# Attention's inverse sums through one 128-column operand, layer 1's map preparation one slot later, the head's tiles in another order

## The chip, the core and the metric

The kernel runs on one core of a Trainium2 chip. Its engines each work through their own list of instructions in order: TensorE (PE) multiplies, VectorE (DVE), ScalarE (ACT) and GpSimd (POOL) work on elements, and SyncE (SP) starts transfers. They meet through semaphores. The metric is the device time of one execution in microseconds (us); 0.2% of it is about what a measurement can tell from no change.

## What is computed

Two layers of a bidirectional encoder over 512 tokens of 1024 channels, in float32. A layer has an attention branch and a state-space branch, both gated, and a feed-forward part (FFN). Cut to what the change touches:

```python
def attend(qi):                       # 8 heads, QK_DIM 96, V_DIM 64
    s = jnp.einsum('bqhd,bkhd->bhqk', qi, k, preferred_element_type=jnp.float32) * scale
    p = jax.nn.softmax(s, axis=-1)
    return jnp.einsum('bhqk,bkhv->bqhv', p.astype(v.dtype), v)

for l in range(DEPTH):                # DEPTH = 2
    ...                               # projections, gates, attention -> branch_a
    y = _s5_bidir(u, ssm_lam_re[l], ssm_lam_im[l], ssm_log_dt[l], ssm_b_re[l], ssm_b_im[l],
                  ssm_c_re[l], ssm_c_im[l], ssm_d[l])
    ...                               # -> branch_b
    x = x + (gate_a * branch_a + gate_b * branch_b) @ w_o[l]
    x = x + _swiglu(_rmsnorm(x, norm2_g[l]), w_ffn_gate[l], w_ffn_up[l], w_ffn_down[l])
```

## The kernel before

**Products.** A float32 product is done as three matmuls (`products`, L1713 to L1715) of high parts and remainders in fp32r. Weights come as slabs of 512 KB: SP loads a slab into `stage`, ACT copies it to `wh` (L603), POOL writes the remainder to `wl` (L511). Transposes and a few small products run in plain float32, where the profile records two passes per matmul.

**Attention.** Four pairs of heads (`hp`), eight units (`u`) a pair: a unit is one head and one block of 128 queries. PE first makes the projected tiles, `qkv_tile(hp, t)`, four a pair (L1984 to L1991). The four transposes `turn(0, i)` of the first pair stand between the tiles of pair 2 and those of pair 3; they wait for POOL's `rotated()` (semaphore `q_ready`) and for the keys. ACT copies each tile (`raw`), and takes roots (`root`); DVE squares and sums, inverts, writes the remainders `turned(0, i)`, then `squares(3)`, and then takes the first maximum.

Then a loop over `a = 8*hp + u` (L1999). In step `a` PE makes the scores of unit `a` (three matmuls), turns the next pair's q and k at `u` 3 to 6 (L1980), transposes the probabilities of unit `a-2` (L2027), and at odd steps multiplies two units' probabilities with the values (L2056, L2057). DVE takes the maximum `nmx` (L1605), the remainder `pTl` (L1621) and others; ACT the exponential `prob` (L1020), the high part `pTh` and others. At `u == 0` DVE inverts the eight sums of the pair that ended (`prc`, L1616). At `u == 1` PE spreads them over bank 6: eight matmuls, each with one column of `prc` broadcast to 64 weight columns and the identity as the moving operand (L2036). ACT copies bank 6 to `Rn` at `u == 2` (`scales`), and POOL scales the output.

POOL's own list in that loop: at `u == 7` `v_rest` (L545, which waits for ACT's `vh_ready`), at `u == 0` of the next pair four products into `rt`, which lies in the tile `SS` (L535), at `u == 1` the two sums L539 and L540, a drain that raises `q_ready`, and the keys `normed_keys` (L552, L555).

**Layer 1's state-space maps** are prepared during layer 0's FFN, in 38 slots: `prepare(l, at)` is called on DVE, ACT and PE after each of the 11 gate/up blocks and each of the 8 output tiles of the two halves. The slots of block of channels `b` follow from `PREP_AT[b]` = 9, 14, 19, 24: DVE's `input_powers` part 0 (L1235 to L1238) in the slot itself, part 1 and `output_powers` part 0 (L1240 to L1284) in the next, `output_powers` part 1 (L1289 to L1294) in the one after, then PE's transposes (L1726) three and four slots on, and the taps (L1741) five on. `input_powers` of block 0 first waits for the store of `TRa` to DRAM (`tr_stored`), which ACT starts in slot 9. Slot 10 follows the last gate/up block of the first half, k = 10. DVE's work of a gate/up block is two products (L1683, L1685), `hid` (L1688) and `hidl` (L1691); PE's output tile m = 0 needs all eleven `hidl`. From m = 2 on, an output tile waits for DVE's addition into `X` (L1700) two tiles back (`x_part`).

Of the kernel before, what the change touches and what calls it, by code (L numbers as in the profile page):

```python
# [12 lines left out]
P = 128  # L13
D_MODEL, SEQ, DEPTH = 1024, 512, 2
HEADS, QK, NOPE, ROPE, VD = 8, 96, 64, 32, 64
# [31 lines left out]
PREP_AT = tuple(9 + 5 * b for b in range(BLOCKS))  # L47
# [31 lines left out]
def build(nc, xT, stream, gcols, gqk, grows, dskip, params, cmat, rope, ident_in, out):  # L79
    with ExitStack() as ctx:  # L80
# [165 lines left out]
        rt = SS[:].rearrange("p (o t h q) -> p o t h q", o=4, t=TT, h=2)  # L246

# [84 lines left out]
        prc_ready = sem("prc_ready")  # L332
        k_normed = sem("k_normed")
# [168 lines left out]
        def _(pool):  # L502
# [11 lines left out]
            for l in range(0, DEPTH):  # L514
# [61 lines left out]
                for a in range(STEPS + 1):  # L576
                    hp, u = a // UNITS, a % UNITS

                    if a < STEPS and hp + 1 < PAIRS:
                        if u == 0:  # L580
                            rotated_products()
                        if u == 1:
                            rotated()
                            normed_keys(hp + 1)
                    elif a < STEPS and u in (2, 4, 6):
                        remainder(SLABS * l + S_UP + u // 2 - 1)
# [14 lines left out]
        def _(act):  # L601
# [149 lines left out]
            def prepare(l, at):  # L751
# [8 lines left out]
                if at == PREP_AT[0]:  # L760
                    store_turns(l)
# [12 lines left out]
            for l in range(0, DEPTH):  # L774
# [214 lines left out]
                for i in range(3 * TT):  # L989
                    raw(i)  # L990
                    if i // TT == 1:
                        squared(i)
                    if i == 5:
                        root(0, 1)
                    if i == 8:
                        v_high(0)
                    if i == 11:
                        root(1, 2)
                for i in range(4):
                    turned(0, i)  # L1000
                for i in range(3 * TT, PAIRS * TT):
                    raw(i)
                for a in range(STEPS + 2):
# [9 lines left out]
                    if a < STEPS:  # L1013
# [4 lines left out]
                        if hp >= 2 and u == 0:  # L1018
                            act.wait_ge(prc_ready, PAIRS * l + hp - 1)
                        act.activation(prob[e][:], ps[:, a % 2, :], ACT.Exp, bias=nmx[:, e:e + 1],  # L1020
                                       accum_out=psm[:, hp % 2, u:u + 1]).then_inc(exp_ready, 1)
                    if a == 4:
                        root(2, PAIRS)
# [9 lines left out]
                    if a >= UNITS and u == 2:  # L1033
                        scales(hp - 1)
# [72 lines left out]
        def _(dve):  # L1107
# [229 lines left out]
            for l in range(0, DEPTH):  # L1337
# [250 lines left out]

                squares(0)
# [9 lines left out]
                for a in range(STEPS + 2):  # L1599
# [17 lines left out]
                    if 2 <= a < STEPS + 2:  # L1617
# [4 lines left out]
                           pTh[o].bitcast(F32), SUB).then_inc(pT_ready, 1)  # L1622
                    if a < STEPS and hp and u == 5:
                        added(hp - 1, 1)
# [85 lines left out]
        def _(pe):  # L1710
# [48 lines left out]
            for l in range(0, DEPTH):  # L1759
# [224 lines left out]
                for hp in range(3):  # L1984
                    for t in range(TT):
                        qkv_tile(hp, t)
# [3 lines left out]
                for t in range(TT):  # L1990
                    qkv_tile(3, t)  # L1991
# [7 lines left out]
                for a in range(STEPS + 4):  # L1999
# [30 lines left out]
                    if a > UNITS and u == 1:  # L2030
# [209 lines left out]
```

## Time and profile before

| | us |
|---|---|
| median of 3 runs | 1555.11 (1554.45 to 1556.94) |
| the profiled execution's own time | 1559.6 |
| its span | 1557.8 |
| PE busy in it | 1520.7 (98%) |
| DVE busy | 872.3 (56%) |
| ACT busy | 601.9 (39%) |
| POOL busy | 579.4 (37%) |

Busy shares are averages over stages. In attention all of PE, DVE and ACT are nearly full; in the FFN PE alone is, save where DVE also prepares layer 1. An idle stretch is read from the engine's own rows: a row of the timeline gives start, duration, engine, line, operation, and in brackets how long the engine sat idle before it and which instruction released it. In such a row `x16` merges sixteen records. Only PE's idle time, and what makes PE slower, can be worth time here.

### The profile page before, as it was taken

What the parts mean: (1) busy time and instruction counts of PE and PEld (TensorE: products, weight loads), DVE (VectorE), ACT (ScalarE), POOL (GpSimd) and SP (SyncE); (2) the same over time, 40 slices, a digit from 0 to 9 for tenths busy, and PEclk for the clock granted to TensorE, in tenths of its full rate; (3) what the DMA queues carried; (4) which work ended last, traced back from release to release, by engine and by line L of the source; (5) the groups of instructions that cost most, each with busy time, mean ns of one, the idle gap of its engine ahead of it and who ended that gap; (6) DMA issues with size and microseconds to landing.
All of it is one profiled execution on the core that took longest, in us unless ns stands there. A gap on an engine that the chain in (4) does not pass through costs nothing.

```text
span 1557.8 us, 20874 instructions
## 1 busy us (share of the span) xinstructions
PE 1520.7 (98%) x8216; PEld 1204.1 (77%) x8216; DVE 872.3 (56%) x1224; ACT 601.9 (39%) x1017; POOL 579.4 (37%) x298
## 2 busy tenths in 40 slices
PE   8999999999999979999999999899999999999999
PEld 3545887878788858788788888787887888888887
DVE  5999877677448876756222971686763222012210
ACT  4554158742442222233332222787334222122220
POOL 0000043454443444354443323445444444443441
PEclk9999999999999989999999999999999999999999
DMA  6568710232232344343528532003223222222222
GB/s 242 165 209 299 276 61 1 69 108 78 90 132 82 118 153 138 121 158 110 163 85 300 207 127 93 28 1 102 100 84 101 89 97 94 94 95 95 95 95 81
DMA packets 73200, 188.32 MB, mean 121 GB/s; under 512 B 23568, under 2 KB 32144, under 8 KB 69008
## 3 DMA queue, kind: packets, MB, share of 16 engines
q1 hardware_dynamic: 41664, 144.13, 27.2%
q10 hardware_dynamic: 31440, 42.87, 8.6%
q8 instruction: 65, 1.06, 0.3%
q14 instruction: 31, 0.25, 0.0%
HBM read 154.47 MB, written 32.51 MB: 120 GB/s over the span
## 4 chain that ended last, share of the span: by engine, by line
PE 76%; DVE 12%; DVEq 5%; ACT 3%; issue 2%; DMA 1%; POOLq 0%; SPq 0%; POOL 0%; ACTq 0%
PE ps L1713 22%; PE ps L1715 22%; PE ps L1714 22%; PE ps L1862 2%; PE ps L2027 1%; DVE work L1115 1%; PE ps L1768 1%; PE ps L1839 1%; DVEq L1295 1%; PE ps L2036 1%; PE ps L2056 1%; PE ps L1807 1%; PE ps L2057 1%; DVEq L1242 1%; ACT prob L1020 1%
## 5 line engine op out<-in xcount | busy, mean ns | idle before, releaser
L511 POOL TENSOR_TENSOR wl<-stage,wh 128x1024 fp32r<-128x1024 f32 x204 | 510.4, 2506 | 872.9 <-ACT wh L603 676.6
L603 ACT ACTIVATE wh<-stage 128x1024 fp32r<-128x1024 f32 x210 | 220.3, 1055 | 320.9 <-PE ps L1715 221.7
L1713 PE MATMUL ps<-xg2h,wh 128*128 128x512 f32 x704 | 279.9, 398 | 0.0
L1715 PE MATMUL ps<-xg2h,wl 128*128 128x512 f32 x704 | 278.4, 395 | 0.0
L1714 PE MATMUL ps<-xg2l,wh 128*128 128x512 f32 x704 | 278.4, 395 | 0.0
L1713 PEld LDWEIGHTS ps<-xg2h,wh 128*128 128x128 f32 x704 | 132.3, 188 | 32.6 <-issue 0.9
L1714 PEld LDWEIGHTS ps<-xg2l,wh 128*128 128x128 f32 x704 | 132.3, 188 | 32.1 <-issue 0.5
L1715 PEld LDWEIGHTS ps<-xg2h,wl 128*128 128x128 f32 x704 | 132.2, 188 | 31.9
L1713 PE MATMUL ps<-hidh,wh 128*128 128x512 f32 x352 | 140.7, 400 | 10.0 <-DVE hidl L1691 9.3
L1714 PE MATMUL ps<-hidl,wh 128*128 128x512 f32 x352 | 139.9, 398 | 0.0
L1715 PE MATMUL ps<-hidh,wl 128*128 128x512 f32 x352 | 139.9, 397 | 0.0
L1700 DVE TENSOR_TENSOR X<-X,ps 128x512 f32<-128x512 f32 x32 | 21.9, 688 | 160.2 <-PE ps L1715 159.8
L1685 DVE TENSOR_TENSOR act<-ps,RS 128x512 f32<-128x512 f32 x44 | 30.3, 689 | 139.4 <-PE ps L1715 139.4
L1768 PE MATMUL ps<-X,slabs 128*128 128x512 f32 x224 | 102.0, 610 | 6.0 <-DMA X<-in_xT 5.1
L603 ACT ACTIVATE hidh<-hid 128x512 fp32r<-128x512 f32 x44 | 27.8, 632 | 164.0 <-DVE hid L1688 164.0
L1768 PEld LDWEIGHTS ps<-X,slabs 128*128 128x128 f32 x224 | 42.5, 194 | 58.7 <-issue 48.4
L1713 PEld LDWEIGHTS ps<-hidh,wh 128*128 128x128 f32 x352 | 66.7, 189 | 26.9 <-DVE hidl L1691 9.7
L1713 PE MATMUL ps<-xgh,wh 128*128 128x512 f32 x208 | 84.4, 406 | 0.0
L1715 PE MATMUL ps<-xgh,wl 128*128 128x512 f32 x208 | 82.3, 396 | 0.0
L1714 PE MATMUL ps<-xgl,wh 128*128 128x512 f32 x208 | 82.3, 395 | 0.0
L1715 PEld LDWEIGHTS ps<-hidh,wl 128*128 128x128 f32 x352 | 66.6, 189 | 16.2
L1714 PEld LDWEIGHTS ps<-hidl,wh 128*128 128x128 f32 x352 | 66.7, 190 | 15.9
(275 smaller groups left out, 2780.4 us busy)
## 6 DMA issues: line engine op xcount, KB each, us to landing
stage<-in_stream SPq DMA_DIRECT2D x210, 512.0 KB, 3.2
CPTR<-ctd_scr ACTq DMA_DIRECT2D x6, 1664.0 KB, 8.1
slabs<-in_stream SPq DMA_DIRECT2D x17, 512.0 KB, 5.7
InT<-in_scr ACTq DMA_DIRECT2D x6, 1024.0 KB, 6.4
ctd_scr<-CPp SPq DMA_DIRECT2D x4, 1152.0 KB, 8.0
ctd_scr<-CPp ACTq DMA_DIRECT2D x4, 1152.0 KB, 6.6
in_scr<-BPI SPq DMA_DIRECT2D x4, 1024.0 KB, 5.1
in_scr<-BPI ACTq DMA_DIRECT2D x4, 1024.0 KB, 3.9
```

Source lines behind the costliest of these rows:

```text
L511: pool.tensor_tensor(wl[:, s, :], stage[:, (n - RAW) % STAGES, :], wh[:, s, :].bitcast(F32), ALU.subtract).then_inc(wl_ready, 1)
L603: return act.activation(o, i, ACT.Copy, **kw)
L1020: act.activation(prob[e][:], ps[:, a % 2, :], ACT.Exp, bias=nmx[:, e:e + 1], accum_out=psm[:, hp % 2, u:u + 1]).then_inc(exp_ready, 1)
L1115: tt(t[0], a[1], b[1], MUL)
L1242: dve.drain()
L1685: tt(act2[:], ps[:, 5 + 2 * b, :], RS[:], MUL).then_inc(ffn_free, 1)
L1700: last = tt(X[:, m, :], X[:, m, :], ps[:, m % 2, :], ADD)
L1713: pe.matmul(o, wt[0], x[0], start=start, stop=False)
L1714: pe.matmul(o, wt[0], x[1], start=False, stop=False)
L1715: return pe.matmul(o, wt[1], x[0], start=False, stop=stop)
L1768: return pe.matmul(o, raw_slab(n)[:, k * P:(k + 1) * P], X[:, k, :], start=start, stop=stop)
L1862: last = pe.matmul(ps[:, 6 + gi, q * NCH:(q + 1) * NCH], CP[h, r, 2 * q + d, at:at + P], S[h, r, 2 * q + d, :], start=False, stop=(d == 1 ...
```

## The change

It has three parts.

1. **Inverse sums.** For the first three pairs of a layer DVE writes a tile `prw`, [128, 4, 128], in the memory of `SS`: `ones` times `prc`, each inverse sum spread over 64 columns, both heads side by side. It does so at `u == 1`, after `pTl`, behind a drain and, for pairs 0 and 1, a wait for `q_ready`, since POOL's `rt` lies in the same memory. PE then makes four float32 matmuls with 128 weight columns at `u == 2` in place of eight with 64 at `u == 1`. ACT's copy to `Rn` moves from `u == 2` to `u == 3`. The last pair is left as it was. POOL waits for `r_ps` before it writes `rt` for pair 3.
2. **Maps.** `PREP_AT` becomes 10, 15, 20, 25; ACT's store of the turns stays in slot 9.
3. **Head.** The first two tiles of pair 3 are made before `turn(0, i)`; ACT copies them before `root(1, 2)`.

```diff
-PREP_AT = tuple(9 + 5 * b for b in range(BLOCKS))
+PREP_AT = tuple(10 + 5 * b for b in range(BLOCKS))
...
+        prw = SS[:].rearrange("p (t c) -> p t c", t=TT)
...
                         if u == 0:
+                            if hp >= 2:
+                                pool.wait_ge(r_ps, PAIRS * l + hp - 1)
                             rotated_products()
...
-                if at == PREP_AT[0]:
+                if at == PREP_AT[0] - 1:
                     store_turns(l)
...
-                    if i == 11:
-                        root(1, 2)
+                for i in range(3 * TT, 3 * TT + 2):
+                    raw(i)
+                root(1, 2)
                 for i in range(4):
                     turned(0, i)
-                for i in range(3 * TT, PAIRS * TT):
+                for i in range(3 * TT + 2, PAIRS * TT):
                     raw(i)
...
+                    if UNITS <= a < STEPS and u == 3:
+                        scales(hp - 1)
...
-                    if a >= UNITS and u == 2:
-                        scales(hp - 1)
...
+                def widened(hp):
+                    if hp + 2 < PAIRS:
+                        dve.wait_ge(q_ready, PAIRS * l + hp + 3)
+                    else:
+                        dve.wait_ge(r_ps, PAIRS * l + hp)
+                    tt(prw.rearrange("p t (h d) -> p t h d", h=2),
+                       ones[:].rearrange("p (h d) -> p h d", h=2)[:, None, :, :].broadcast_to([P, TT, 2, VD]),
+                       prc[:, hp % 2, :].rearrange("p (h t) -> p t h", h=2)[:, :, :, None].broadcast_to([P, TT, 2, VD]),
+                       MUL).then_inc(prc_wide, 1)
...
+                    if a < STEPS and hp and u == 1:
+                        dve.drain()
+                        widened(hp - 1)
...
-                for hp in range(3):
-                    for t in range(TT):
-                        qkv_tile(hp, t)
+                for i in range(3 * TT + 2):
+                    qkv_tile(i // TT, i % TT)
                 pe.wait_ge(qk_sqa, TT * (l + 1))
                 for i in range(4):
                     turn(0, i)
-                for t in range(TT):
+                for t in range(2, TT):
                     qkv_tile(3, t)
...
-                    if a > UNITS and u == 1:
+                    if UNITS <= a < STEPS and u == 2:
+                        pe.wait_ge(prc_wide, 3 * l + hp)
+                        pe.wait_ge(qkT_ready, 4 * n)
+                        for t in range(TT):
+                            last = pe.matmul(ps[:, 6, t * P:(t + 1) * P], prw[:, t, :], ident, start=True, stop=True)
+                        last.then_inc(r_ps, 1)
+                    if a > STEPS and u == 1:
```

How the instructions then stand, from the order of the built programs (a row: line, operation, what it writes and reads, and the semaphores it waits for).

DVE before, from the end of gate/up block 9 in the first FFN half of layer 0 (`act`, `hid`, `hidl` are a block's work, `BPI` and `work` the preparation's):

```order
L1691 TENSOR_TENSOR hidl<-hid,hidh 128x512 [waits hidh_ready]
L1235 TENSOR_TENSOR BPI_96<-BB_88,pwi_90 128x1024 [waits tr_stored]
L1236 TENSOR_TENSOR BPI_96<-BB_88,pwi_90 128x1024
L1237 TENSOR_TENSOR work_94<-BB_88,pwi_90 128x1024
L1238 TENSOR_TENSOR work_94<-BB_88,pwi_90 128x1024
L1683 TENSOR_TENSOR act_132<-ps,RS 128x512 [waits slab_done]
L1685 TENSOR_TENSOR act_133<-ps,RS 128x512 [waits slab_done]
L1688 TENSOR_TENSOR hid<-act_132,act_133 128x512 [waits silu_ready]
L1691 TENSOR_TENSOR hidl<-hid,hidh 128x512 [waits hidh_ready]
L1240 TENSOR_TENSOR BPI_96<-BPI_96,work_94 128x1024
```

The same place in the changed kernel, whose line numbers are higher:

```order
L1709 TENSOR_TENSOR hidl<-hid,hidh 128x512 [waits hidh_ready]
L1701 TENSOR_TENSOR act_132<-ps,RS 128x512 [waits slab_done]
L1703 TENSOR_TENSOR act_133<-ps,RS 128x512 [waits slab_done]
L1706 TENSOR_TENSOR hid<-act_132,act_133 128x512 [waits silu_ready]
L1709 TENSOR_TENSOR hidl<-hid,hidh 128x512 [waits hidh_ready]
L1240 TENSOR_TENSOR BPI_96<-BB_88,pwi_90 128x1024 [waits tr_stored]
L1241 TENSOR_TENSOR BPI_96<-BB_88,pwi_90 128x1024
L1242 TENSOR_TENSOR work_94<-BB_88,pwi_90 128x1024
L1243 TENSOR_TENSOR work_94<-BB_88,pwi_90 128x1024
L1718 TENSOR_TENSOR X<-X,ps 128x512 [waits down_done]
L1245 TENSOR_TENSOR BPI_96<-BPI_96,work_94 128x1024
```

The four input powers now stand behind block 10's `hidl` and ahead of the first addition into `X`.

PE before, in the attention loop of layer 0 at step `a = 9` (pair 1, `u == 1`), up to the scores of `a = 10`:

```order
L2027 MATMUL ps<-identm,prob_112 128x128 [waits pT_ready,exp_ready]
L2027 MATMUL ps<-identm,prob_112 128x128 x3
L2036 MATMUL ps<-identm,prc 64x128 [waits qkT_ready,prc_ready]
L2036 MATMUL ps<-identm,prc 64x128 x7
L2056 MATMUL ps<-pTh,vv_105 128x256 [waits pT_ready]
```

The changed kernel, from the scores of `a = 10` to those of `a = 11` (`SS` is the spread tile):

```order
L1731 MATMUL ps<-qkTh_119 128x512 [waits exp_ready]
L1732 MATMUL ps<-qkTl_121,qkTh_119 128x512
L1733 MATMUL ps<-qkTh_119,qkTl_121 128x512
L2044 MATMUL ps<-identm,prob_113 128x128 [waits pT_ready,exp_ready]
L2044 MATMUL ps<-identm,prob_113 128x128 x3
L2051 MATMUL ps<-identm,SS 128x128 [waits qkT_ready,prc_wide]
L2051 MATMUL ps<-identm,SS 128x128 x3
L1731 MATMUL ps<-qkTh_119 128x512 [waits exp_ready]
```

The eight matmuls left `a = 9`, and four wider ones stand in `a = 10` behind a wait for DVE.

DVE in the changed kernel over the same two steps:

```order
L1631 RECIPROCAL prc<-psm 128x8 [waits exp_ready]
L1636 TENSOR_TENSOR pTl<-ps,pTh 128x4x128 [waits pTh_ready]
L1620 TENSOR_REDUCE nmx<-ps 128x1 [waits score_ps]
L1636 TENSOR_TENSOR pTl<-ps,pTh 128x4x128 [waits pTh_ready]
L1599 TENSOR_TENSOR SS<-ones,prc 128x512 [waits q_ready]
L1620 TENSOR_REDUCE nmx<-ps 128x1 [waits score_ps]
```

L1599 is new; the maximum of `a = 10` is now queued behind it and its wait.

## Rows read from the trace of the kernel before

**Rows 1.** The page: busy time and share of the span of each engine.

```profile
PE 1520.7 (98%) x8216; PEld 1204.1 (77%) x8216; DVE 872.3 (56%) x1224; ACT 601.9 (39%) x1017; POOL 579.4 (37%) x298
```

**Rows 2.** PE's waits in the whole span, second line: total us, times, longest.

```profile
PE ps L1713 <- ACT prob L1020: 6.5, 10, 1.4
```

**Rows 3.** Timeline of PE, 538 to 600 us: start, duration, what, [idle before].

```profile
546.42 0.39 PE L1715 MATMUL ps<-hidh,wl 128*128 128x512 f32 x1
556.11 0.80 PE L1713 MATMUL ps<-hidh,wh 128*128 128x512 f32 x1 [9.30 <-DVE hidl L1691]
...
560.12 0.56 PE L1713 MATMUL ps<-hidh,wh 128*128 128x512 f32 x1
...
568.30 0.50 PE L1713 MATMUL ps<-hidh,wh 128*128 128x512 f32 x1 [0.68 <-DVE X L1700]
...
576.10 1.03 PE L1726 MATMUL ps<-identm,BPI 128*128 128x128 f32 x8
576.89 0.48 PE L1713 MATMUL ps<-hidh,wh 128*128 128x512 f32 x1
```

**Rows 4.** Timeline of DVE over the same stretch.

```profile
547.89 1.23 DVE L1235 TENSOR_TENSOR BPI<-BB,pwi 128x1024 f32<-128x1024 f32 x1 [6.09 <-DMA ctd_scr<-TRa]
...
553.98 0.69 DVE L1688 TENSOR_TENSOR hid<-act,act 128x512 f32<-128x512 f32 x1
555.37 0.69 DVE L1691 TENSOR_TENSOR hidl<-hid,hidh 128x512 fp32r<-128x512 f32 x1 [0.70 <-ACT hidh L603]
...
567.55 0.69 DVE L1700 TENSOR_TENSOR X<-X,ps 128x512 f32<-128x512 f32 x1
...
575.77 1.29 DVE L1700 TENSOR_TENSOR X<-X,ps 128x512 f32<-128x512 f32 x2
```

**Rows 5.** Timelines of ACT and of POOL over the same stretch.

```profile
541.49 2.01 ACT L603 ACTIVATE wh<-stage 128x1024 fp32r<-128x1024 f32 x2 [0.42 <-issue]
...
542.62 4.75 POOL L511 TENSOR_TENSOR wl<-stage,wh 128x1024 fp32r<-128x1024 f32 x2 [6.92 <-ACT wh L603]
```

**Rows 6.** Timeline of DVE, 600 to 700 us, in the second half.

```profile
632.66 1.22 DVE L1235 TENSOR_TENSOR BPI<-BB,pwi 128x1024 f32<-128x1024 f32 x1
...
641.75 0.69 DVE L1683 TENSOR_TENSOR act<-ps,RS 128x512 f32<-128x512 f32 x1
...
667.23 2.12 DVE L1691 TENSOR_TENSOR hidl<-hid,hidh 128x512 fp32r<-128x512 f32 x1 [0.70 <-ACT hidh L603]
```

**Rows 7.** Head of layer 0's attention: timelines of PE and of DVE.

```profile
223.56 0.61 PE L1980 MATMUL ps<-identm,QW 128*96 128x128 f32 x4 [1.87 <-POOLq L541]
...
232.32 0.50 PE L1713 MATMUL ps<-qkTh 96*128 96x512 f32 x1 [1.36 <-ACT prob L1020]
...
230.17 0.49 DVE L1538 TENSOR_TENSOR qks<-ps,qkv 128x320 f32<-128x320 f32 x1 [0.47 <-ACT qkv L603]
230.76 1.29 DVE L1605 TENSOR_REDUCE nmx<-ps 128x1 f32<-128x512 f32 x2
```

**Rows 8.** Busy time by window, PEclk the granted clock's share (seventh figure).

```profile
232.00:236.00 4.00, 3.68 (x13) 2.88 (x14) 3.16 (x7) 2.20 (x7) 0.00 (x0) 0.60 0.00 0
```

**Rows 9.** The loop, pair 1, layer 0: timelines of PE, DVE, POOL.

```profile
249.76 1.58 PE L2036 MATMUL ps<-identm,prc 128*64 128x128 f32 x16
251.27 0.38 PE L2056 MATMUL ps<-pTh,vv 128*128 128x256 f32 x1
...
253.38 0.48 PE L1713 MATMUL ps<-qkTh 96*128 96x512 f32 x1
...
250.67 0.69 DVE L1621 TENSOR_TENSOR pTl<-ps,pTh 128x512 fp32r<-128x512 f32 x1
...
252.50 0.46 POOL L540 TENSOR_TENSOR QW<-SS 128x128 f32<-128x128 f32 x1
253.14 1.04 POOL L552 TENSOR_TENSOR KW__117<-qkv,ast 128x512 f32<-128x512 f32 x1 [0.18 <-issue]
```

**Rows 10.** DVE's key product at 219 us, two operands in SBUF, 256 elements.

```profile
219.08 1.69 DVE L1562 TENSOR_TENSOR KW__117<-KR,ast 128x256 f32<-128x256 f32 x1
```

More of the change, by code:

```diff
@@ L332, in build @@
         prc_ready = sem("prc_ready")
+        prc_wide = sem("prc_wide")
         k_normed = sem("k_normed")
```

## The prediction

> **What bounds the kernel now.** I read the page's busy shares first: PE is busy for 98% of the span, the others for 56% and less [rows 1]. So an edit is worth only what it takes out of PE's own rows or out of PE's idle time. Then I read PE's waits. One stands out: before the matmul at 556.11 us PE sat idle for 9.30 us, released by DVE's `hidl` [rows 3]. Ten more waits, 6.5 us in all, are for ACT's `prob` in attention [rows 2], 0.65 each. The reader should then look at DVE over the large wait: it stood still for 6.09 us until the store of `TRa` had landed at 547.89, ran four input powers, and only then did block 10's work [rows 4]. The last thing to ask is what DVE, ACT and POOL do around the two edits in attention, where the edits put DVE behind POOL.
>
> **Part 2, the maps a slot later.** Removed: the idle 9.30 us, and the slow matmuls behind it. From 556.11 to 560.12 PE made 9 matmuls in 4.01 us [rows 3], where nine take 2.1 at the usual pace (tile 2's 33 matmuls ran from 568.30 to 576.10, 0.236 us each [rows 3]); 1.9 us lost. The small wait of 0.68 for `X` [rows 3] belongs to the same backlog and goes too. Together 11.9 us.
>
> What comes in its place, step by step.
> - Block 10. ACT is in its two slab copies until 541.49 + 2.01 = 543.50 [rows 5], then takes the silu (some 0.65 us, an estimate from half a slab copy's 1.0 and `hid`'s 0.69), so `hid` can start at about 544.17. From the start of `hid` to PE's matmul it took 556.11 - 553.98 = 2.13 us [rows 3, 4]: PE could go on at 546.30, and it needs this at 546.42 + 0.24 = 546.66. No wait, if nothing is in the way. But POOL works from 542.62 to 547.37 [rows 5], and a `hidl` in such a place took 2.12 instead of 0.69 us [rows 6], 1.4 more. I take a wait of 1.4 - 0.35 = 1.1 us; bounds 0 and 2.1 (both `hid` and `hidl` held up, less the slack).
> - The input powers now run after that, from about 548. Four at 1.23 are at most 4.9 us undisturbed [rows 4]; beside POOL the same four took 641.75 - 632.66 = 9.1 [rows 6]. Until they end, DVE doesn't make the addition of tile 0 into `X`, for which PE's tile 2 waits. A tile is 33 matmuls, 7.8 us, so PE comes there at 539.6 + 15.6 + 1.1 = 556.3 us (tile 0 began 30 matmuls, 7.0 us, ahead of 546.66). DVE starts the addition at 557.1, PE goes on 568.30 - 567.55 = 0.75 later [rows 3, 4], at 557.9: a wait of 1.6, bounds 0 and 2.
> - Then part 1 and the first output powers: 567.55 - 556.06 = 11.5 us before [rows 4], of which a good part was POOL; by the powers' example I take 9.1, to 557.7 + 9.1 = 566.8. PE's tile 3 is due at 557.9 + 7.8 + 0.8 (eight transposes, 576.89 - 576.10 [rows 3]) = 566.5 and gets `X` at 567.6: 1.1, bounds 0 and 3.6. The last four (575.77 - 567.55, less 0.6 for the addition, 7.6 [rows 4]) end at 575.0, and tile 4 is due at 576.2: no wait.
>
> Sum of the new waits 1.1 + 1.6 + 1.1 = 3.8, bounds 0 and 7.7. **Part 2: -11.9 + 3.8 = -8.1 us**, between -11.9 and -4.2. Moved with it and hidden: PE's transposes and taps (same count), ACT's copies, the three kinds of store that ACT starts a slot later; in the second half DVE's last preparation ends in slot 26 and the last `hidl` stands in slot 29, and by the change it ends in slot 27, still two blocks ahead. The store of the turns isn't moved, so the landing at 547.89 is no longer what PE waits for.
>
> **Part 3, the head.** PE's idle 1.87 us before `turn(0, 0)` [rows 7] is filled by two tiles. But behind the turns stands DVE: `turned(0, i)`, `squares(3)`, the first maximum, and PE's third unit waits for the exponential of the first. In this chain only DVE's wait of 0.47 for ACT's copy of the last tile [rows 7] goes; its start depends on pair 2's tiles, which aren't moved. So the 1.87 us turn up as a longer wait for `prob` at 232.32, and 0.5 us per layer are gained. **Part 3: -1.0 us** for both layers, bounds 0 and -3.7 (all of the idle time).
>
> **Part 1, the inverse sums.** Removed at each of six places: sixteen records, 251.27 - 249.76 = 1.51 us [rows 9]. Added: four matmuls in two passes, eight records. Nearest rows: eight transposes with 128 weight columns and 128 moving ones, 0.79 us [rows 3]; half of the sixteen, 0.76 us [rows 9]. I take 0.8; PE's own work falls by 0.7 a place, 4.2 in all. That is the gain if the operand is there in time.
>
> It isn't for pairs 0 and 1. DVE's spread waits for `q_ready`. POOL ended L540 at 252.96 and went on at 253.14 [rows 9]; the raising of `q_ready` lies between the two. So the spread starts at 253.15, takes 0.69 (DVE's usual for 512 elements, as its `pTl` [rows 9]), and with 0.1 for the semaphore PE may start at 253.94 and is done at 254.74. Without the eight matmuls PE has made the scores of `a = 10` and the transposes by 253.38 - 1.51 = 251.87: it waits 2.1 us. The scores of `a = 11` then start at 254.74 instead of 253.38 [rows 9], 1.36 us later than before. The same distances hold in pair 2 and in layer 1, so four places of 1.36. PE's later waits for `prob` (0.65 each [rows 2]) can absorb little of it, since ACT is set back as well: its next copy needs PE's transposes, and `Rn` now stands in the step where ACT also copies `qkTh`. I take 0.1 as absorbed: +1.26 each, 5.0 in all.
>
> Then there is who goes first at 253.15. POOL's L552 starts at 253.14 [rows 9], a hundredth of a microsecond from the spread. DVE's L1562 took 1.69 us for 256 elements beside a POOL operation [rows 10], where 512 take 0.69; so if POOL is first, the spread ends only after L552's 1.04 us. That is 0 or +1.0 at each of four places; I take the half, +2.1.
>
> For this the Trainium skill has a rule (SBUF — State Buffer, "Who interferes with whom"): a VectorE instruction with two SBUF inputs contends with a GpSimd instruction that reads SBUF, and whichever starts first keeps the pair for the whole instruction. L1562 agrees with it. By the rule the term is 0 or 1.04 at each place and nothing between; were there no contention, part 1 would be 2.1 us less.
>
> The third place of a layer waits for nothing of POOL's. DVE's `pTl` ends at 251.36 in this pattern [rows 9]; the spread, 252.15; PE, there at 251.87, waits 0.3 to 0.4 and loses half of the gain. I take 0 for both, bounds -0.7 and +0.3. **Part 1: 5.0 + 2.1 + 0 = +7.1 us**, between -4.2 (operand in time everywhere) and +9.7.
>
> **Sum.** -8.1 - 1.0 + 7.1 = -2.0 us on the profiled execution's 1559.6. That execution is 4.5 us above the median of the runs shown; the terms are stretches of PE and don't depend on that, so I take them off the median: 1555.1 - 2.0 = **1553.1 us**, -0.13%.
>
> **Rivals.**
> - *The spread is no wait.* DVE, ACT and PE are each full in the loop, and a later PE may find DVE and ACT without their own gaps, so that the 2.1 us of waiting replace waits that would come anyway. For it: the ten waits for `prob`. Against: they sum to 6.5 us, and part of them lies in the head. Part 1 then is between -4.2 and 0, say -2: -8.1 - 1.0 - 2 = -11.1, 1544.0 us. Chance 0.2.
> - *FFN clean.* DVE's powers fall between POOL's slabs: part 2 is -11.9 and POOL loses the tie at 253.15 (part 1 +5.0): -11.9 - 1.0 + 5.0 = -7.9, 1547.2 us. Chance 0.12.
> - *The wait turns into one for `X`.* DVE has the same work for block 0's maps, now ahead of the first three additions; at the upper bounds the new waits are 7.7, part 2 is -4.2: -4.2 - 1.0 + 7.1 = +1.9, 1557.0 us. Decided by how many of DVE's twelve operations meet a POOL slab. Chance 0.15.
> - *Slower: the clock falls in attention.* Behind a wait of 1.36 us PE's granted clock was 0.60 of 2.4 GHz over 4 us [rows 7, 8], so in good part at the lower level, 1.2 GHz; these 4 us cost some 1.6. The change makes four waits of 2.1 to 3.1 us and one of some 3 in each head. If the clock falls behind three of them and POOL wins the tie everywhere (+2.0 more), the sum is -2.0 + 2.0 + 3 x 1.6 = +4.8, 1559.9 us. Against it: behind the 1.87 us idle in the head the next rows ran at the usual pace. It decides from the point where such a wait is enough. Chance 0.13.
>
> **How the numbers follow.** The forecast has 0.40; its own range is -5 to +2 us (tie lost or won everywhere, part 2 within 2). A difference of 0.2%, 3.1 us, is about what a measurement of this kernel tells from no change. Faster by more: 0.2 + 0.12 and a fifth of the forecast's 0.40, together 0.40. Slower by more: 0.13, some of the `X` rival, a little of the forecast: 0.19. Within: 0.41. Range for 8 in 10: from 1545.5, which leaves out half of the first rival, to 1559.5, which leaves out half of the slow one.
>
> **What the changed profile would show.** Right for part 2: no wait on `hidl` near 546 us beyond 2, and waits on `X` of 1 to 2 before tiles 2 and 3. Right for part 1: eight records of some 0.8 us in place of sixteen of 1.51, DVE idle before the spread for 1.2 to 1.8 us released by POOL's queue, and four waits of PE near 2 us for the spread; the spread either 0.69 or about 1.7 long. Right for part 3: `turn(0, 0)` without a wait, the first wait for `prob` near 3 us. It is wrong if PE's waits for the spread are under 1 us, if the loop of a pair doesn't grow by about 1.3 us while the spread waits for POOL, or if PE's clock row falls below 1.0 between 249 and 300 us.

## Result and the profile after

The changed kernel took **1564.02 us** (median of 4 runs, 1562.47 to 1564.80) where the kernel before took 1554.78 beside it: a ratio of 1.0051, 95% interval 1.0038 to 1.0064 (the ratios here are estimates over all runs, not quotients of the two medians). A second set of 6 runs gave 1563.4 against 1555.5, 1.0048 (1.0031 to 1.0065). The forecast was 1553.1, with a range up to 1559.5: the kernel is slower, and by more than the range allows. The profiled execution took 1563.94 us, its span is 1562.1.

PE's waits, summed over the span (us in total, times, longest), answer to [rows 2, 3]:

```profile
PE ps L1731 <- ACT prob L1025: 10.2, 10, 2.8
PE ps L2051 <- DVE SS L1599: 9.2, 6, 1.9
...
PE ps L1731 <- DVE X L1718: 1.7, 1, 1.7
PE ps L1731 <- DVE hidl L1709: 1.6, 1, 1.6
```

The wait of 9.30 for `hidl` is 1.6 now. The new line is the second: six waits for the spread of the inverse sums, 9.2 us. And the waits for `prob` grew from 6.5 to 10.2; 2.9 of these 3.7 us are the two heads, where a wait of 2.83 stands in place of one of 1.36.

The place in pair 1 of layer 0 that answers to [rows 9], PE first, then DVE, then POOL:

```profile
249.88 0.60 PE L2044 MATMUL ps<-identm,prob 128*128 128x128 f32 x4
252.35 1.89 PE L2051 MATMUL ps<-identm,SS 128*128 128x128 f32 x8 [1.87 <-DVE SS L1599]
253.89 0.77 PE L1731 MATMUL ps<-qkTh 96*128 96x512 f32 x1
254.46 0.63 PE L1732 MATMUL ps<-qkTl,qkTh 96*128 96x512 f32 x1
```

```profile
251.60 0.69 DVE L1599 TENSOR_TENSOR SS<-ones,prc 128x512 f32<-128x512 f32 x1 [1.68 <-POOLq L543]
```

```profile
251.70 1.50 POOL L554 TENSOR_TENSOR KW__117<-qkv,ast 128x512 f32<-128x512 f32 x1 [0.18 <-issue]
```

DVE waits 1.68 us for POOL's queue and PE 1.87 us for DVE: that is as foretold. But the eight records then take 1.54 us to the next scores, not 0.8, and the first matmul of these scores takes 0.77 where it took 0.48 [rows 9]. That is the clock, which stood at half speed:

```profile
252.00:254.00 2.00, 1.65 (x9) 0.64 0.00 0
254.00:256.00 2.00, 2.00 (x9) 0.50 0.00 0
```

The wider windows of PE (window, its length, PE's busy time and records, then the granted clock as a share of 2.4 GHz, DMA share, GB/s), first of the changed kernel, then of the kernel before:

```profile
228.00:240.00 12.00, 8.78 (x48) 0.86 0.00 0
248.00:262.00 14.00, 11.94 (x77) 0.88 0.00 1
270.00:282.00 12.00, 9.93 (x60) 0.86 0.01 1
994.00:1006.00 12.00, 9.16 (x50) 0.86 0.00 0
1018.00:1030.00 12.00, 9.94 (x70) 1.00 0.00 0
1038.00:1050.00 12.00, 9.94 (x63) 0.86 0.00 0
```

```profile
228.00:240.00 12.00, 9.86 (x52) 0.86 0.00 0
248.00:262.00 14.00, 14.00 (x105) 1.00 0.00 1
270.00:282.00 12.00, 11.59 (x83) 1.00 0.00 1
994.00:1006.00 12.00, 10.63 (x77) 1.00 0.00 0
1018.00:1030.00 12.00, 12.00 (x92) 1.00 0.00 0
1038.00:1050.00 12.00, 11.60 (x84) 1.00 0.01 1
```

Both kernels lose the clock in the head of layer 0 (228 to 240). The changed one loses it in the head of layer 1 (994) as well, and behind three of the four waits in pairs 1 and 2. The prediction had named this as a sign of being wrong: a clock below 1.0 between 249 and 300 us. The time from the first scores of a layer's attention to its last, read from PE's timeline, is 66.11 and 65.35 us before, 74.25 and 72.95 after.

The FFN stretch that answers to [rows 3 to 5]: PE, DVE, POOL.

```profile
553.88 0.50 PE L1731 MATMUL ps<-hidh,wh 128*128 128x512 f32 x1 [1.62 <-DVE hidl L1709]
...
572.82 0.50 PE L1731 MATMUL ps<-hidh,wh 128*128 128x512 f32 x1 [1.71 <-DVE X L1718]
```

```profile
549.51 1.53 DVE L1706 TENSOR_TENSOR hid<-act,act 128x512 f32<-128x512 f32 x1 [1.06 <-ACT act L1088]
551.74 2.09 DVE L1709 TENSOR_TENSOR hidl<-hid,hidh 128x512 fp32r<-128x512 f32 x1 [0.70 <-ACT hidh L607]
553.75 1.21 DVE L1240 TENSOR_TENSOR BPI<-BB,pwi 128x1024 f32<-128x1024 f32 x1
...
560.66 0.69 DVE L1718 TENSOR_TENSOR X<-X,ps 128x512 f32<-128x512 f32 x1
...
572.08 0.69 DVE L1718 TENSOR_TENSOR X<-X,ps 128x512 f32<-128x512 f32 x1
```

```profile
548.08 5.19 POOL L513 TENSOR_TENSOR wl<-stage,wh 128x1024 fp32r<-128x1024 f32 x2 [6.92 <-ACT wh L607]
```

This part behaves as foretold: `hid` and `hidl` are held up by POOL's slabs and PE waits 1.62 us; the input powers follow; one wait for `X`. And the head of layer 0, answering to [rows 7]: no wait before `turn(0, 0)`, one long one before the third unit's scores, and slow matmuls from 231.89 on.

```profile
231.09 0.50 PE L1731 MATMUL ps<-qkTh 96*128 96x512 f32 x1 [2.83 <-ACT prob L1025]
...
231.89 0.85 PE L2044 MATMUL ps<-identm,prob 128*128 128x128 f32 x4
232.40 0.78 PE L1731 MATMUL ps<-qkTh 96*128 96x512 f32 x1
```

### The profile page after: what moved, and what is told of

Same layout as the page of the kernel before. It is cut to its first block, busy times and chain, and to the rows that moved or that the text cites. A ratio compares the mean times of both kernels' runs of the same rounds, so it can differ in the third digit from the quotient of the medians.

```text
span 1562.1 us, 20790 instructions
## 1 busy us (share of the span) xinstructions
PE 1523.1 (98%) x8168; PEld 1206.8 (77%) x8168; DVE 889.8 (57%) x1230; ACT 601.9 (39%) x1017; POOL 582.2 (37%) x298
## 4 chain that ended last, share of the span: by engine, by line
PE 73%; DVE 14%; DVEq 5%; ACT 4%; issue 3%; POOLq 1%; DMA 1%; POOL 1%; SPq 0%; ACTq 0%
PE ps L1731 22%; PE ps L1732 22%; PE ps L1733 22%; PE ps L1880 2%; DVE work L1120 1%; PE ps L1786 1%; PE ps L1857 1%; DVEq L1300 1%; ACT prob L1025 1%; DVEq L1247 1%; PE ps L1825 1%; DVE qkTl L1574 1%; DVE nmx L1620 1%; PE ps L2051 1%; PE ps L2044 1%
```

## The experiments

Theory A: the loss is in the edit of the inverse sums, and it has two parts, the waits themselves and the lower clock behind them. Theory B: it comes from how the parts act on each other, or from the wide products and the moved copy. Later expectations split theory A: the "clock theory" says that the lower clock behind PE's waits costs, the "order theory" counts only what the new order of the instructions costs or saves. Twelve kernels, four at a time beside the kernel before (medians 1556.04, 1556.35 and 1555.51 us in the three sets); a difference is taken from the median beside it. One thing must be known to read them. The same kernel's runs differ by up to 8 us, and with them the mean granted clock: the 67 runs of the kernel before go from 1553.0 us at 0.997 to 1561.1 at 0.992, about 1.2 us for each 0.001. So beside each median stands the mean clock of its runs. The kernel before has 0.9947, the changed one (its 10 runs) 0.9908.

A table ahead of the single experiments: the distances between starts of scores on PE's timeline, in us, layer 0 / layer 1 (units 0, 8, 16, 24 and 31). They hold no DMA wait and nothing of the rest of the kernel.

| kernel | head (0 to 8) | pair 1 (to 16) | pair 2 (to 24) | pair 3 (to 31) |
|---|---|---|---|---|
| before | 17.78 / 17.01 | 16.80 / 16.80 | 17.83 / 17.83 | 13.70 / 13.71 |
| changed | 19.03 / 19.32 | 20.12 / 18.50 | 20.70 / 20.75 | 14.40 / 14.38 |
| changed_again | 18.90 / 20.38 | 19.88 / 19.82 | 20.55 / 20.41 | 14.39 / 14.39 |
| sums_only | 17.79 / 17.74 | 18.47 / 18.48 | 20.70 / 20.61 | 14.39 / 14.40 |
| half_fed | 19.26 / 19.03 | 18.51 / 18.50 | 19.10 / 19.14 | 14.39 / 14.39 |
| all_fed | 18.48 / 18.46 | 18.49 / 18.50 | 19.12 / 19.13 | 14.39 / 14.40 |
| own_place | 18.47 / 19.25 | 17.26 / 17.25 | 18.34 / 18.34 | 14.21 / 14.21 |
| own_first | 19.04 / 20.39 | 16.55 / 16.56 | 18.28 / 18.27 | 13.72 / 13.73 |
| head_fed | 18.48 / 18.49 | 16.79 / 16.78 | 17.83 / 17.83 | 13.65 / 13.66 |
| maps_fed | 17.00 / 17.00 | 16.82 / 16.80 | 17.83 / 17.81 | 13.69 / 13.70 |

The values in a column fall into a few sharp steps, and the granted clock in the windows of PE tells which cells hold a fall of the clock.

### The parts alone

maps_only, the kernel before with

```
-PREP_AT = tuple(9 + 5 * b for b in range(BLOCKS))
+PREP_AT = tuple(10 + 5 * b for b in range(BLOCKS))
-                if at == PREP_AT[0]:
+                if at == PREP_AT[0] - 1:
                     store_turns(l)
```

> The kernel before with the maps a slot later and nothing else. The forecast had -8.1 us for it. Order theory: about 1556.0 - 8 to -9 = 1547 to 1548, the FFN's idle 9.3 us replaced by waits of 1.6 and 1.7, and the heads as before, with PE's waits of 1.87 and 1.36 there. If the gain of the maps is smaller than its places say: 1550 or more.

Measured 1548.19 us (6 runs), ratio 0.9944 (0.9927 to 0.996), mean clock 0.998: -8.2 us. By place, from the last scores of layer 0 to the first of layer 1, it is 691.22 us where sums_only, with the old maps, has 700.02: -8.8. PE's two waits in place of the 9.30:

```profile
548.56 0.50 PE L1713 MATMUL ps<-hidh,wh 128*128 128x512 f32 x1 [1.55 <-DVE hidl L1691]
567.51 0.50 PE L1713 MATMUL ps<-hidh,wh 128*128 128x512 f32 x1 [1.71 <-DVE X L1700]
```

head_only, the kernel before with the tiles of the head moved:

```
-                for hp in range(3):
-                    for t in range(TT):
-                        qkv_tile(hp, t)
+                for i in range(3 * TT + 2):
+                    qkv_tile(i // TT, i % TT)
...
-                for t in range(TT):
+                for t in range(2, TT):
                     qkv_tile(3, t)
```

and ACT's copies and root in the matching order.

> The kernel before with the head's tiles moved and nothing else: in each layer PE's waits of 1.87 and 1.36 us become one of 2.8. The forecast had -1.0 us. Clock theory: the longer wait makes the clock fall in both layers' heads more often than the two short ones did (in the run without the sums' edit it fell there twice, 6.8 us at the lower level, against 3.4 us in the kernel before), so the time is 1556 - 1.0 + 1.7 to 3.4 = 1557 to 1559. Order theory alone: 1555.

Measured 1554.87 us (12 runs), ratio 0.9992 (0.9979 to 1.0006), mean clock 0.994: -1.5 us, not to be told from no change. By place the order gives 0.5 a layer: the first scores stand 3.8 us behind `turn(0, 0)` instead of 5.8, and the head behind them is 1.5 longer without a fall (18.48 in head_fed, 17.00 in maps_fed). The clock theory's 1557 to 1559 was wrong for this kernel: in its profile the clock fell once in each head, 1.7 us of clock lost in each, where the kernel before has that in layer 0's alone, and its runs' mean clock is 0.001 lower; that isn't enough to undo the gain.

sums_only, the kernel before with `widened`, the four wide products and `scales` a unit later, and nothing else.

> The kernel before with the edit of the inverse sums alone. Theory A: 1554.8 + (1564.0 - 1545.3) = about 1573, with waits of 1.9, 1.9 and 0.9 us per layer for the spread and the clock falling behind at least three of them. Theory B (interaction: a part of the loss arises only with the moved head tiles): 1562 or less, what my forecast had for this part (+7.1).

Measured 1568.74 us (6 runs), ratio 1.0084 (1.0066 to 1.0101), mean clock 0.991: +12.7 us. Theory A said 1573, B 1562 or less; it lies between, nearer to A. PE's waits for the spread are the same as in the changed kernel, 9.1 us in six places.

maps_and_head, the changed kernel without the sums' edit.

> The kernel before with the maps a slot later and the head's tiles moved, without the edit of the inverse sums. Theory A (the loss is all in the inverse sums: their four waits on POOL and what they bring on): the changed kernel's FFN halves gained some 8.6 us by the places of the additions into X, the head 0.5 a layer, so 1554.8 - 9.5 = about 1545.3, and no clock fall in attention outside the heads. Theory B (the moved head tiles or the maps cost in layer 1, where the new clock fall at 1000 to 1004 us stands in the head): the gain is much smaller, 1550 or more, and the fall in layer 1's head is there.

Measured 1550.21 us (10 runs), ratio 0.9959 (0.9946 to 0.9973), mean clock 0.994: -5.8, where theory A's 1545.3 was a gain of 9.5 and theory B's 1550 one of 4.8 or less. It lies nearer to B, and B's sign, a fall in layer 1's head, is there. So not all of the loss lies in the sums' edit. Its profile shows where the rest is. In its two heads the clock stayed down twice as long as in head_only's: 12 x (1 - 0.72) and 16 x (1 - 0.79) us, 3.4 each, are lost by the first pair of rows below. (Its profile also has a fall in the scan of layer 1, of which more at the end, and those of maps_only and head_only have none.)

### The heads' wait filled

head_fed is maps_and_head with

```
+                        if a == 2:
+                            pe.wait_ge(qkT_ready, 4 * n + 3)
+                            for t in range(3 * TT):
+                                pe.matmul(ps[:, 2, t % TT * P:(t % TT + 1) * P], ident, ident, start=True, stop=True)
                         if a >= 2:
                             pe.wait_ge(exp_ready, at - 1)
```

The added products go to a bank that the next transposes overwrite.

> Maps a slot later and head's tiles moved, without the sums' edit, and with twelve added products of the identity with itself (2.4 us) in each head's wait of 2.84 us. Clock theory: no clock fall in either head, where the kernel without them had 3.4 us lost at the lower level in each; 1550.2 - 3 to -6 = 1544 to 1547. Rival (the falls there are no matter of PE's idle time): 1550 or more, the added products only in the way.

Windows of PE, maps_and_head, then head_fed; then head_fed's timeline of PE in layer 0:

```profile
228.00:240.00 12.00, 9.14 (x38) 0.72 0.00 0
984.00:1000.00 16.00, 13.16 (x75) 0.79 0.00 0
```

```profile
228.00:240.00 12.00, 10.37 (x73) 1.00 0.00 0
984.00:1000.00 16.00, 14.36 (x102) 1.00 0.01 2
```

```profile
228.41 2.84 PE L2010 MATMUL ps<-identm 128*128 128x128 f32 x24
231.42 0.50 PE L1714 MATMUL ps<-qkTh 96*128 96x512 f32 x1 [0.16 <-ACT prob L1021]
```

Measured 1548.15 us (6 runs), ratio 0.9941 (0.9926 to 0.9956), mean clock 0.998. The falls in both heads are gone, and each head is 1.7 to 1.8 us shorter than in maps_and_head (20.19 and 20.33 there, 18.48 and 18.49 here), though PE does 24 records more. The clock theory had said 1544 to 1547 and the rival 1550 or more: the falls went as it said, and the median is 1.2 us above its range. It ties with maps_only for the lowest median of the study.

maps_fed is maps_only with added products in the two waits of the old head (eight and six).

> The kernel before with the maps a slot later, and added products in the head's two waits (1.6 us in the 1.87, 1.2 us in the 1.36). maps_only had falls behind them, one of 1.7 us in each layer, in its profiled run: 1548.2 - 2 = 1546 if they go. If the median stays at 1548, most of its runs had none there already.

Measured 1549.33 us (6 runs, 1544.98 to 1550.20), ratio 0.9951 (0.9935 to 0.9967). Its heads are 17.00 us in both layers, the shortest of all, yet the median isn't under maps_only's: four of its six runs have a clock of 0.997 to 0.998, and in the profiled one the clock fell in the scan of layer 1, near 882 to 894 us, which neither edit touches. The two runs at a clock of 1.000 took 1545.0 and 1546.4.

### The waits for the spread filled

filled_wait is the changed kernel with eight more products in pairs 1 and 2, four in pair 3:

```
+                        pe.wait_ge(qkT_ready, 4 * n)
+                        for t in range(2 * TT if hp + 1 < PAIRS else TT):
+                            pe.matmul(ps[:, 6, t % TT * P:(t % TT + 1) * P], ident, ident, start=True, stop=True)
                         pe.wait_ge(prc_wide, 3 * l + hp)
-                        pe.wait_ge(qkT_ready, 4 * n)
```

> The changed kernel with eight more products of the identity with itself ahead of PE's wait for the spread (four in the third pair of heads), into the bank that the real products then overwrite: PE works in the 1.9 us in which it stood idle, and the real products start when they did. It parts the wait from the clock. Clock theory: the granted clock stays at 1.00 at 252 to 256, 272 to 278 and 1040 to 1046 us, the eight records take 0.8 instead of 1.54, and the kernel is 4 to 6 us faster than the changed one (three falls of some 1.6 us each, worked out from the kernel before), at 1558 to 1560. If the clock is not what costs: 1564, or later by what the added products overrun, up to 2 us.

Measured 1558.51 us (12 runs), ratio 1.0008 (0.9995 to 1.0021), mean clock 0.996: 5 to 6 us under the changed kernel, as the clock theory said, though nothing waits less and PE has 40 products more.

half_fed has four products (0.8 us) in each place, so that about 1.0 us stays idle.

> The changed kernel with four added products (0.8 us) ahead of each wait for the spread, so that 1.1 us of idle stay in pairs 1 and 2. If idle of 1.1 us is still enough to bring the clock down: 1563 to 1564, falls behind pairs 1 and 2 as in the changed kernel. If it isn't: as with 1.6 us filled, 1558 to 1559, no falls there.

Measured 1557.61 us (12 runs), ratio 1.0008 (0.9996 to 1.0021), mean clock 0.996. PE in pair 1 of layer 0, then the windows of the four places:

```profile
250.85 1.06 PE L2050 MATMUL ps<-identm 128*128 128x128 f32 x8
252.88 1.16 PE L2053 MATMUL ps<-identm,SS 128*128 128x128 f32 x8 [0.97 <-DVE SS L1599]
253.80 0.48 PE L1731 MATMUL ps<-qkTh 96*128 96x512 f32 x1
```

```profile
248.00:262.00 14.00, 12.84 (x94) 1.00 0.00 1
270.00:282.00 12.00, 10.85 (x80) 1.00 0.00 1
...
1018.00:1030.00 12.00, 11.33 (x78) 1.00 0.00 1
1038.00:1050.00 12.00, 11.44 (x80) 1.00 0.01 2
```

With half of the idle filled the clock stays up, and the eight records take 0.92 us (252.88 to 253.80) instead of 1.54. Pair 2 is 19.10 instead of 20.70: 1.6 us for a fall.

all_fed has the products of filled_wait and of head_fed.

> The changed kernel with added products of the identity in both kinds of wait: 2.4 us in each head's wait of 2.84, 1.6 us in the waits of 1.9 and 0.8 us in those of 0.9 for the spread. Clock theory: with no fall left in attention the sum of the forecast's three terms holds, 1556 - 8.2 - 1.5 + 7.3 = about 1553.5 or a little less (the kernel before has falls of its own in the head). Rival: 1558 as with the sums' waits alone filled.

Measured 1556.34 us (12 runs, 1552.80 to 1559.08), ratio 0.9998 (0.9984 to 1.0011), mean clock 0.998. This is 2.8 us more than the clock theory's 1553.5, about halfway to the rival's 1558. Its three runs at a clock of 1.000 took 1552.8, 1553.3 and 1553.7. The others have 0.997 to 0.998; the profiled one is among them, and there all six windows of attention stand at 1.00 and the clock fell in the scan of layer 1.

changed_again is the changed kernel.

> The changed kernel as it is, timed beside the other three so that they stand on the same chip: 1564, with a mean granted clock near 0.991, where the kernel before has 0.992 to 0.997. If its clock spreads as widely as that of the kernel before, the first four times were one-sided, and the loss by the clock is smaller than the 6 us that the filled waits gave back.

Measured 1563.4 us (6 runs), clock 0.989 to 0.991 in five of them and 0.996 in one, which took 1558.87. In its profile the clock fell behind all four waits of pairs 1 and 2, while the first profile had it at 1.00 behind the one at 1021 us, after the same idle of 1.87. Its windows:

```profile
248.00:262.00 14.00, 12.14 (x76) 0.88 0.01 1
...
1018.00:1030.00 12.00, 10.24 (x62) 0.86 0.00 0
```

### The wait itself taken away

own_place gives the spread its own memory, in the part of the projections that is no longer read, so that it needn't wait for POOL to leave `SS`:

```
-        prw = SS[:].rearrange("p (t c) -> p t c", t=TT)
+        PRW = spare.take("PRW", [P, SEQ])
+        prw = PRW[:].rearrange("p (t c) -> p t c", t=TT)
...
-                    if hp + 2 < PAIRS:
-                        dve.wait_ge(q_ready, PAIRS * l + hp + 3)
+                    if hp:
+                        dve.wait_ge(r_ps, PAIRS * l + hp)
                     else:
-                        dve.wait_ge(r_ps, PAIRS * l + hp)
+                        dve.wait_ge(v_ready, PAIRS * l + 2)
```

> The changed kernel, but VectorE's spread operand has its own place in memory (the part of the first heads' projections that is no longer read), so that it doesn't share the one in which POOL keeps its rotated products, and waits for none of them. Everything else, the order of all instructions too, is as in the changed kernel. Theory A (the loss is the wait for POOL and the clock falls behind it): the spread runs at once after the maximum's neighbour, some 1.7 us earlier, PE's 9.2 us of waits for it go to under 2, the clock stays up in attention, and the eight records cost 0.8 where sixteen cost 1.5: 1554.8 - 9.5 - 3 = about 1542; at least 15 us under the changed kernel. Theory B (the loss comes from the wide products or from the moved copy of ACT, not from the wait): stays within 4 us of the changed kernel's 1564.0.

Measured 1552.20 us (12 runs), ratio 0.9979 (0.9965 to 0.9994), mean clock 0.995: 11 to 12 us under the changed kernel. No window of pairs 1 to 3 is below 1.00 any more. But it isn't the 1542 of theory A: PE still waits 0.62 to 0.9 us at each place.

```profile
PE ps L2050 <- DVE PRW L1598: 4.7, 6, 0.9
```

own_first has VectorE make the spread ahead of the step's low half instead of behind it.

> The changed kernel with the spread in its own place, and VectorE making it ahead of that step's low half instead of behind it, 0.7 us earlier. PE's waits for it (4.7 us in six places) should go below 1. If PE alone bounds the loop, the time falls by about 4 us, 1552.2 to 1548. If VectorE is as full as PE there, the low half that is now 0.7 us later gives the wait to the exponentials and the turns, and the time stays at 1551 to 1553.

Measured 1551.05 us (6 runs), ratio 0.9954 (0.9937 to 0.9972), mean clock 0.996. The view of the line of the spread says that nobody waits for it:

```profile
L1598 DVE TENSOR_TENSOR PRW<-ones,prc x6: 692/848/859, 249.2 to 1047.5; 128x512 f32<-128x512 f32 x6
its engine sat idle before it (us, times) until:
who waited for it (us, times):
```

(The three numbers are the shortest, middle and longest duration of the spread, in ns.) And yet the three pairs take 16.55 + 18.28 + 13.72 = 48.55 us where head_fed, with the old sixteen products, takes 16.79 + 17.83 + 13.65 = 48.27. With the operand in time everywhere the edit gains nothing. PE's own work is 0.6 us a place shorter (1.51 less 0.92), 1.8 a layer. Against it, its waits from 248 us to the end of layer 0's attention are 3.5 us where head_fed has 2.3: 1.1 for `qkTl` instead of 0.4, 0.4 for `Rn` instead of none, the rest for `prob`. The other 0.9 us aren't located. That these waits come from DVE, which has 0.69 to 0.86 us more in each pair, and from ACT's copy of `Rn` in the step where it also copies `qkTh`, is argued and not shown. Nor are DVE and ACT as full there as was said ahead of the prediction: from 262 to 296 us of the kernel before DVE is busy for 27.2 of 34 us, ACT for 30.6, PE for 32.4.

## Why the prediction was wrong

**Part 2 was right.** Forecast -8.1, measured -8.2 alone and -8.8 by place. Its steps: the wait for `hidl` was put at 1.1 with only `hidl` held up by POOL; both were, and it was 1.6. The input powers were given 9.1 us by an example with more POOL work; they took 6.9 (553.75 to 560.66), so that tile 2 waited for nothing, and tile 3 waited 1.7 instead of 1.1. New waits 3.3 against 3.8. (The upper bound of 2.1 for the first wait doesn't follow from its terms: twice 1.4 less 0.35 is 2.45, so the `X` rival's 7.7 would be 8.0. Nothing else hangs on it.)

**Part 3 was right by place.** Forecast -1.0; the -1.5 measured alone can't be told from nothing. The heads without a fall show it cleanly: 18.48 against 17.00, 1.48 longer, with the first scores 2.0 us earlier, so -0.5 a layer. What it did beside that was to make one idle of 2.83 of two of 1.87 and 1.36, and the profiled run of the changed kernel had a fall in the head of layer 1 that the kernel before didn't have. The two shorter waits are no safe place either: with the old head the clock fell in five of six heads (before, sums_only, maps_only), with the long wait unfilled in fifteen of sixteen.

**Part 1's order was right, its clock wasn't there.** Without falls (all_fed against head_fed, pairs 1 to 3) it costs 18.49 - 16.79 = 1.7, 19.12 - 17.83 = 1.3 and 14.39 - 13.65 = 0.7: 3.7 a layer, 7.5 in both. The forecast was 7.1, and that the totals agree is in good part luck, since its terms miss both ways: the wait of 1.87 (foretold 2.1) and the 1.36 a place hold, the tie with POOL was won every time, so that the 2.1 us for it weren't there, and the third pair, put at 0, cost 0.7 a layer, because PE waited 0.9 there and not 0.3 to 0.4. A further 0.4 in pair 1 stands between units 12 and 13 (1.89 us where it was 1.50), where PE's transposes of the keys wait 0.2 for `Rn`.

On the tie, the profile shows all six spreads at 0.69 us, while POOL's operation, which started 0.10 us after the first of them, took 1.50 instead of the 1.04 of before. The rule cited in the prediction from the Trainium skill (SBUF — State Buffer, "Who interferes with whom") agrees: the one that starts first keeps the pair, and here that was VectorE. In size it is near: 0.59 us of the spread were left when POOL's operation started, and it took 0.46 longer.

**The step that failed is the clock.** The forecast's sum has no term for PE's clock: the forecast left it out and gave it to a rival, with three falls of 1.6 us and a chance of 0.13, "against it: behind the 1.87 us idle in the head the next rows ran at the usual pace". That one row was taken as a rule. The profile of maps_only has the same wait in the same place, and there the clock is at half speed right behind it (the transposes took 0.61 before):

```profile
222.90 1.06 PE L1980 MATMUL ps<-identm,QW 128*96 128x128 f32 x4 [1.88 <-POOLq L541]
```

The changed kernel makes the same idle four more times, and the clock fell behind three of them in one profile and behind four in the other; a fall costs 1.3 to 1.6 us where it stands (table: 20.12 against 18.50 in pair 1, 20.70 against 19.10 in pair 2). Summed over attention, the changed kernel is 74.25 + 72.95 = 147.2 us where all_fed is 70.48 + 70.49 = 141.0: 6.2 us of clock, 7.8 in the second profile. The kernel before has 0.8 (131.46 against 130.65 in maps_fed).

The sum then is -8.2 for the maps, -1.1 for the heads' order, +7.5 for the sums' order and +5.4 to +7.0 for the clock in attention, +3.6 to +5.2 in all. The two profiled spans differ by 1562.1 - 1557.8 = 4.3. By place on PE's timeline these 4.3 are -2.7 up to layer 0's first scores, +8.1 in its attention, -8.7 from there to layer 1's first scores, +7.6 in its attention, and nothing behind it.

The medians differ by 8 to 9, because the profiled run of the kernel before was a slow one of its kind: 1559.6, 4.5 us above its median. Most of this 4.5 can be seen in its profile. It lost 0.8 in the head of layer 0, and it lost the clock in the scan of layer 1 (PE's 64 x 64 products of the state-space branch), which no edit touches. What such a fall costs is read from the stretch between the two attentions. In the kernels with the new maps and the new head it is 689.6 or 689.7 us where the scan has no fall (half_fed, filled_wait), 692.3 to 692.7 with 3.4 us of clock lost (maps_and_head, head_fed, changed_again) and 694.3 to 694.4 with 5.1 (the changed kernel, all_fed, own_place, own_first): 2.7 to 3.1 us and 4.7 us. The kernel before, with 3.4 lost, has 703.02 where sums_only, with none, has 700.02: 3.0 us, so 3.8 with the head's. The rows of PE there, half_fed, then the changed kernel:

```profile
887.51 3.79 PE L1880 MATMUL ps<-S,CPTR 64*128 64x64 f32 x64 [1.09 <-DVE S L1444]
890.22 6.54 PE L1880 MATMUL ps<-S,CPTR 64*128 64x64 f32 x64 [1.09 <-DVE S L1444]
```

The same wait stands before both, so its length doesn't decide there. It is open what does, and how often each kernel loses the clock in this place: none was lost in the profiles of sums_only, maps_only, head_only, filled_wait and half_fed, and no order of the edits explains it. No run here was made to settle it.

The nearest thing to a run of the forecast's own world is all_fed at a clock of 1.000: 1552.8 to 1553.7 us. So 1553.1 is near the time of this kernel when its clock doesn't fall, and the changed kernel is not that one. Even this is partly luck: the forecast started from a median with the falls of the kernel before in it, and all_fed at a mean clock of 1.000 can have next to none anywhere, in the scan neither. The first rival (the spread is no wait) is refuted twice, by the 9.2 us and by own_first, in which even its absence brings no gain. The slower rival named the mechanism and its place; its price was too low (1559.9 against 1564.0) because it had three falls, where the profiles have five and six stretches of lower clock in attention, the heads with them, and it also carried 2.0 us for POOL winning the tie, which never came.

## What to carry to other kernels

Price an idle stretch of PE not by its length alone, but as its length plus a chance of a fall of the clock. Look at the granted clock behind every idle of that length in the trace, not behind one: here 1.9 us of waiting cost another 1.3 to 1.6 in nine cases of twelve. Before an operation is made shorter for PE, ask what other engine must make its operand, and in which memory: the wide operand cost DVE 0.69 us where PE saved 0.6, and its place in `SS` tied it to POOL. Where an idle of 2 us can't be taken away, a few products that nobody reads are a cheap way to keep the clock, and here half of the idle was enough. Where runs of one kernel differ with the mean clock, find in the profile which stretch pays for it before the medians are compared.

## What the runs showed of the hardware

A wait of 1.87 us on PE in the otherwise full pairs 1 and 2 brought its granted clock down to 1.2 GHz (0.50 at 254 to 256 us), with 1.7 us of clock lost each time (14 x 0.12 and 12 x 0.14 in the windows), in nine places of twelve: three of four in the first profile of the changed kernel, four of four in the second, two of four in sums_only's; with 0.97 us left idle it never fell in four places (half_fed), nor in the eight with all of it filled (filled_wait, all_fed). The same instruction stream, with the same 1.87 us, kept it once at 1021 us and lost it there in another run. In the scan of layer 1 a wait of 0.73 to 1.13 us stood before the 64 products in every profile, and the clock fell in nine of fourteen. The Trainium skill (TensorE: Matmul & The Clock Gate, "Why this matters for your kernels") warns of longer idle stretches than these only; the rows here show that shorter ones do it as well. And the differences of up to 8 us between runs of one program on one core go with its granted clock: 0.997 for the shortest, 0.992 for the longest of the 67 runs of the kernel before.
